# Output projection in four passes of four weight units, and the softmax exponential taken head by head from the score banks

## What is computed

```
h = rms_norm(x); proj = h @ w_in
A  y_conv = gb * conv3(gc * a)                       256 wide
B  y_attn = sliding-window attention, 8 heads of 64  512 wide
     m = max(max(scores), sink); e = exp(scores - m)
     p = e / (sum(e) + exp(sink - m))
C  y_gmlp = gelu(u) * (W_s @ layer_norm(gelu(v)) + b)  256 wide
x = x + concat(rms_norm(A), rms_norm(B), rms_norm(C)) @ w_out
x = x + square(relu(rms_norm(x) @ w_ff1)) @ w_ff2
```

## Time and profile before

| | us |
|---|---|
| median of 3 runs | 2534.04 |
| lowest and highest run | 2528.53, 2535.17 |
| the profiled execution | 2527.28 |
| its span, first to last instruction | 2525.3 |
| PE busy in the span | 2421.5 |
| DVE busy | 1244.2 |
| ACT busy | 609.3 |
| POOL busy | 115.0 |

### The profile page before, as it was taken

One profiled execution on the slowest core, in us unless ns is written; L12 is line 12 of the kernel. 1 busy time (PEld: TensorE's weight loads), 2 busy tenths in 40 slices (PEclk: granted clock), 3 DMA queues, 4 the chain that ended last, 5 costly groups with the idle time before them and its releaser, 6 DMA issues.

```text
span 2525.3 us, 35462 instructions
## 1 busy us (share of the span) xinstructions
PE 2421.5 (96%) x13094; PEld 2138.9 (85%) x13094; DVE 1244.2 (49%) x2221; ACT 609.3 (24%) x1281; POOL 115.0 (5%) x223
## 2 busy tenths in 40 slices
PE   7998998999999999999989998899999999999998
PEld 6987776988998899889888876679899889988996
DVE  5236755444444444444462477464444444444446
ACT  4123412321222122212231234133122212221222
POOL 4010000000000000000020100010000000000001
PEclk9999998999999999999999998999999999999999
DMA  5111001111111111111020011001111111111111
GB/s 159 35 30 42 28 16 34 51 42 43 50 33 38 45 50 33 39 44 58 17 66 26 31 42 35 29 22 59 42 50 33 42 42 50 33 42 42 50 34 75
DMA packets 121189, 109.11 MB, mean 43 GB/s; under 512 B 9724, under 2 KB 93216, under 8 KB 121104
## 3 DMA queue, kind: packets, MB, share of 16 engines
q1 hardware_dynamic: 117248, 100.66, 13.3%
q0 software_dynamic: 2704, 3.10, 0.5%
q10 hardware_dynamic: 1152, 4.19, 0.4%
HBM read 102.18 MB, written 5.54 MB: 43 GB/s over the span
## 4 chain that ended last, share of the span: by engine, by line
PE 89%; DVE 5%; DMA 3%; ACT 2%; issue 1%; SPq 0%; POOL 0%; DVEq 0%; ACTq 0%; POOLq 0%
PE ps L1180 28%; PE ps L1182 28%; PE ps L1181 28%; DMA w_raw<-in_w_out 2%; PE ps L1223 1%; DVE w_lo L830 1%; PE ps L1364 1%; PE ps L1327 1%; PE ps L1347 1%; DVE hT_lo L854 0%; DVE hT_lo L964 0%; SPq L343 0%; PE ps L1308 0%; DVE xn L848 0%; ACT w_hi L552 0%
## 5 line engine op out<-in xcount | busy, mean ns | idle before, releaser
L1180 PE MATMUL ps<-hT_hi,w_hi 128*128 128x384 f32 x1824 | 619.1, 339 | 4.2 <-DVE hT_lo L854 4.2
L1181 PE MATMUL ps<-hT_lo,w_hi 128*128 128x384 f32 x1824 | 616.9, 338 | 0.0
L1182 PE MATMUL ps<-hT_hi,w_lo 128*128 128x384 f32 x1824 | 616.8, 338 | 0.0
L1026 DVE TENSOR_TENSOR x<-ps,x 128x512 f32<-128x512 f32 x576 | 398.1, 691 | 299.5 <-PE ps L1182 290.3
L1180 PE MATMUL ps<-w_hi,ff_hi 128*128 128x512 f32 x1152 | 460.5, 400 | 0.0
L1182 PE MATMUL ps<-w_hi,ff_lo 128*128 128x512 f32 x1152 | 455.7, 396 | 0.0
L1181 PE MATMUL ps<-w_lo,ff_hi 128*128 128x512 f32 x1152 | 452.6, 393 | 0.0
L993 DVE TENSOR_TENSOR r_sb<-r_sb 128x384 f32<-128x384 f32 x192 | 107.0, 558 | 556.1 <-ACT r_sb L611 556.1
L1180 PEld LDWEIGHTS ps<-hT_hi,w_hi 128*128 128x128 f32 x1824 | 345.1, 189 | 6.4 <-DVE hT_lo L854 4.6
L1181 PEld LDWEIGHTS ps<-hT_lo,w_hi 128*128 128x128 f32 x1824 | 345.1, 189 | 1.2
L1182 PEld LDWEIGHTS ps<-hT_hi,w_lo 128*128 128x128 f32 x1824 | 344.8, 189 | 0.0
(11 more groups left out here) (164 smaller groups left out, 1717.3 us busy)
## 6 DMA issues: line engine op xcount, KB each, us to landing
w_raw<-in_w_ff SPq DMA_DIRECT2D x256, 256.0 KB
w_raw<-in_w_in SPq DMA_DIRECT2D x56, 256.0 KB
w_raw<-in_w_out SPq DMA_DIRECT2D x32, 256.0 KB
out<-xn SPq DMA_DIRECT2D x9, 512.0 KB, 2.6
x<-in_x_prompt ACTq DMA_DIRECT2D x7, 512.0 KB, 10.5
w_raw<-in_w_in SPq DMA_DIRECT2D x16, 128.0 KB
gN<-in_w_norm SPq DMA_DIRECT2D x2, 512.0 KB, 6.9
gN<-in_w_norm POOLq DMA_DIRECT2D x2, 512.0 KB, 3.9
```

What stands on the lines that cost most here:

```text
L1026: V.tensor_tensor(xv, ps[:, 6 + n, :], xv, ALU.add).then_inc(x_added.sem, 1)
L1180: pe.matmul(out, sh, mh, start=first, stop=False)
L1181: pe.matmul(out, sh, ml, start=False, stop=False)
L1182: return pe.matmul(out, sl, mh, start=False, stop=last)
```

## The change

The projection is cut by groups and column halves: first the groups A and C ("sides", two units each) of column half 0 for all tiles, then those of half 1, then group B ("attn", four units) of half 0, then of half 1. The units are laid out in this order, so that each part uses four consecutive units. `project_out` is replaced by `side_rows` and `attn_rows` on TensorE and by `add_sides` and `add_attn` on VectorE. The order around the last query tiles is written out anew; the splits of units 44 to 47 come after the adds of side tile 5, the others one by one behind later adds. The last part runs with the second norm. The norm's banks change, and `ff1(0)` takes groups 0 and 1 of its second chunk before it waits for the norm's last tile.

In the softmax VectorE makes `nb = -max/8` instead of subtracting. ScalarE reads the scores from their banks, one call for each head with `nb` as bias, writes `S`, and gives the row sums into `den`. The next scores wait for the exponentials.

```diff
         def norm_banks(w, t):
-            first = (0, 2)[t % 2] if w == 1 else (3, 5)[t % 2]
+            first = (0, 2)[t % 2] if w == 1 else (6, 4)[t % 2]
...
-                        w = HEADS * P if t < TS else DEC_BATCH * KEYS_S
+                        w = P if t < TS else KEYS_S
                         act.wait_ge(*s_sub.at(t))
-                        nc.scalar.activation(S[:, t % 2, 0:w], S[:, t % 2, 0:w], ACT.Exp, scale=SC).then_inc(
-                            *exp_done.tick((t, 0)))
+                        for h in range(HEADS):
+                            nc.scalar.activation(S[:, t % 2, h * w:(h + 1) * w],
+                                                 ps[:, 3 + h // 4, (h % 4) * w:(h % 4 + 1) * w], ACT.Exp,
+                                                 bias=nb[:, h:h + 1], scale=SC,
+                                                 accum_out=den[:, h:h + 1]).then_inc(*exp_done.tick((t, h)))
                         nc.scalar.activation(es[:], sd[:], ACT.Exp, scale=SC).then_inc(*exp_done.tick(t))
                     if i == TS:
 
                         copy_qT(TS)
+                    if i == T + 1:
                         split(range(U_OUT + 4, U_OUT + 8))
...
-                V.tensor_tensor(s_view(t, w), v, by_head(mx[:], w), ALU.subtract)
+                V.tensor_scalar(nb[:], mx[:], -SC, None, ALU.mult)
                 V.tensor_tensor(sd[:], sink[:, kind, :], mx[:], ALU.subtract).then_inc(*s_sub.tick(t))
...
-                link(V.tensor_reduce(den[:].rearrange("p (b h) -> p b h", b=2), s_view(t, w), AX_X, ALU.add))
```

VectorE, after the query tiles:

```diff
+                add_sides(0, 0)
+                softmax_max(TS)
+                add_sides(0, 1)
+                mixed_rows(TS - 2)
+                value_rows(TS - 1)
+                add_sides(0, 2)
+                softmax_norm(TS)
+                add_sides(0, 3)
+                mixed_low(TS - 2)
+                group_scale(TS - 3)
+
+                mixed_rows(TS - 1)
+                add_sides(0, 4)
+                mixed_low(TS - 1)
+                group_scale(TS - 2)
+                add_sides(0, 5)
+                split(range(U_OUT + 4, U_OUT + 8))
+
+                mixed_rows(TS)
+                add_sides(0, 6)
+                mixed_low(TS)
+                group_scale(TS - 1)
+                add_sides(0, 7)
+                group_scale(TS)
+                add_sides(0, TS)
+
+                for t in range(T):
+                    add_sides(1, t)
+                    if 1 <= t <= 4:
+                        split([U_OUT + 8 + t - 1])
+                for t in range(T):
+                    add_attn(0, t)
+                    if 1 <= t <= 4:
+                        split([U_OUT + 12 + t - 1])
                 for t in range(T + 2):
-                    if t == TS:
-                        split(range(U_FF, U_FF + 2))
                     if t < T:
-                        project_out(1, t)
+                        add_attn(1, t)
                     if 1 <= t <= T:
                         normalise(2, t - 1)
                     if t >= 2:
                         norm_low(2, t - 2)
-                    if t == TS:
-                        split(range(U_FF + 2, U_FF + 4))
+                    if 2 <= t <= 5:
+                        split([U_FF + t - 2])
```

TensorE, in `scores`, and the new helpers:

```diff
-                    pe.wait_ge(*s_sub.at(t - 1))
+                    pe.wait_ge(*exp_done.at(t - 1))
...
+            def out_bank(q):
+                if q >= 2:
+                    pe.wait_ge(*out_acc.at(q - 2))
+                else:
+                    pe.wait_ge(*(qn_raw, qT_done)[q].at(TS))
+                return ps[:, (0, 2)[q % 2], :]
+
+            def side_rows(n, t):
+                if n == 0:
+                    pe.wait_ge(*mix_lo.at(t))
+                for grp, ks in enumerate(((0, 1), (6, 7))):
+                    q = side_index(n, t, grp)
+                    ins = rows_by_cols(out_bank(q), t, U_OUT + 4 * n, ks, at=2 * grp)
                     if t < TS:
                         ins.then_inc(*out_full.tick(q))
+
+            def attn_rows(n, t):
+                q = attn_index(n, t)
+                ins = rows_by_cols(out_bank(q), t, U_OUT + 8 + 4 * n, (2, 3, 4, 5), at=0)
```

TensorE, after the query tiles:

```diff
+                q_turn(TS)
+                scores(TS)
+                side_rows(0, 0)
+                values(TS - 2)
+                p_turn(TS - 1)
+                group_sums(TS - 3)
+                for t in (1, 2, 3):
+                    side_rows(0, t)
+
+                values(TS - 1)
+                p_turn(TS)
+                group_sums(TS - 2)
+                side_rows(0, 4)
+                side_rows(0, 5)
+
+                values(TS)
+                group_sums(TS - 1)
+                side_rows(0, 6)
+                group_sums(TS)
+                side_rows(0, 7)
+                side_rows(0, TS)
+
+                for t in range(T):
+                    side_rows(1, t)
+                for t in range(T):
+                    attn_rows(0, t)
                 for t in range(T + 2):
                     if t < T:
-                        project_out(1, t)
+                        attn_rows(1, t)
                     if t >= T:
 
                         g = t - T
-                        pe.wait_ge(*out_acc.at(out_index(1, TS, 2)))
+                        pe.wait_ge(*out_acc.at(attn_index(1, TS)))
                         pe.wait_ge(*norm_lo.at((2, 3 * g + 2, 1)))
                         ff1(0, groups=(g,), chunks=(0,))
                     if t >= 2:
                         norm_turn(2, t - 2)
                 pe.wait_ge(*norm_lo.at((2, TS - 1, 1)))
+                ff1(0, groups=(0, 1), chunks=(1,))
                 pe.wait_ge(*norm_lo.at((2, TS, 1)))
-                ff1(0, groups=(2,), chunks=(0,))
-                ff1(0, chunks=(1,))
+                ff1(0, groups=(2,))
```

More of the change, by code:

```diff
@@ L285, in tile, with side_index, attn_index @@
             return slice(t * P, (t + 1) * P)
-        def out_index(n, t, grp):
-            return (n * T + t) * 3 + grp
+        def side_index(n, t, grp):
+            return (n * T + t) * 2 + grp
+        def attn_index(n, t):
+            return 4 * T + n * T + t
         def y_count(b, t, n):
@@ L415, in _ @@
                     load(vs[64:80, b, :], v_sb[16 * b:16 * b + 16, TS, :], vs_in, "last")
-                for n in range(2):
-                    for k in range(KD):
-                        i = real(U_OUT + n * KD + k)
-                        cols = slice(n * 512, n * 512 + 512)
-                        if 2 <= k < 6:
-                            src = w_out[bass.ds(l, 1), 256:768, cols].rearrange(
-                                "l (g h d) e -> h (l g) d e", g=2, h=G4)[k - 2]
-                        else:
-                            src = out_rows[bass.ds(l * D + k * P, P), cols]
-                        unit(i, 0, raw[:, i % RAW, :], src)
+                for part in range(2):
+                    for n in range(2):
+                        for j in range(4):
+                            i = real(U_OUT + 8 * part + 4 * n + j)
+                            cols = slice(n * 512, n * 512 + 512)
+                            if part == 1:
+                                src = w_out[bass.ds(l, 1), 256:768, cols].rearrange(
+                                    "l (g h d) e -> h (l g) d e", g=2, h=G4)[j]
+                            else:
+                                src = out_rows[bass.ds(l * D + (0, 1, 6, 7)[j] * P, P), cols]
+                            unit(i, 0, raw[:, i % RAW, :], src)
                 w1_units(real(ids_of_w1(0)), 0, 0)
@@ L966, in mixed_low, with add_rows, add_sides, add_attn @@
                 last.then_inc(*mix_lo.tick(t))
-            def project_out(n, t):
-                for grp in range(3):
-                    q = out_index(n, t, grp)
-                    unit = U_OUT + 8 * n + (1, 5, 7)[grp]
-                    if n == 0 and t == TS:
-                        split(range(U_OUT + 8 + (0, 2, 6)[grp], U_OUT + 8 + (2, 6, 8)[grp]))
-                    dve.wait_ge(*(out_full.at(q) if t < TS else released(unit)))
-                    dve.wait_ge(*rg_done.at(t))
-                    if q >= 1:
-                        dve.wait_ge(*out_acc.at(q - 1))
-                    V.scalar_tensor_tensor(x[:, t, n * 512:n * 512 + 512], ps[:, (0, 2)[q % 2], :],
-                                           rG[:, t, grp:grp + 1], x[:, t, n * 512:n * 512 + 512], ALU.mult,
-                                           ALU.add).then_inc(*out_acc.tick(q))
+            def add_rows(n, t, q, grp, unit, ready):
+                dve.wait_ge(*(out_full.at(q) if t < TS else released(unit)))
+                dve.wait_ge(*rg_done.at(t))
+                if ready is not None:
+                    dve.wait_ge(*out_acc.at(ready))
+                xv = x[:, t, n * 512:n * 512 + 512]
+                V.scalar_tensor_tensor(xv, ps[:, (0, 2)[q % 2], :], rG[:, t, grp:grp + 1], xv, ALU.mult,
+                                       ALU.add).then_inc(*out_acc.tick(q))
```

(29 more changed lines are left out.)

87 lines of the change are left out of this document (26 added, 61 removed).

## The result

The changed kernel took 2488.69 us as the median of 4 runs (2485.01 to 2494.01); the kernel before took 2532.84 us in 4 runs beside it. The ratio is 0.983, with a 95% interval of 0.981 to 0.9849: faster by 1.7%. The profiled execution took 2487.94 us, against 2527.28 before: 39.3 us less, where 38.8 was forecast. In a later comparison the changed kernel took 2492.13 us (2490.85 to 2493.58), ratio 0.984 (0.9827 to 0.9852).

A forecast was written before the change was run, and what follows sets the result against it. TensorE, busy 96% of the span, bounds the kernel; only its idle time and half clock can be won. Removing 29.9 us a layer less 10.5 of new losses nets 38.8: 2488.5 profiled, median 2495, range 2479 to 2508.

The forecast's parts named there:

- my bounds of 2.3 and 3.9: ScalarE's eight exponential calls a tile: 2.3 us with overlap, 3.9 without; the middle, 3.1, was taken.
- tightest query copy: Query loop: the exponential ends 1.1 us later, the tightest copy's slack is 0.68, so TensorE waits 0.45 once a layer.
- last query copy, beyond before: Last query tile: TensorE already waited for this copy, and that wait grows by 1.15 us a layer.
- (a): Group sums of tile 8 wait for VectorE's late group scale of tile 7: 2.7 us idle, 1.7 more of clock.
- (b): Last pass with the second norm: VectorE and ScalarE rounds outlast TensorE's tiles; 3.1 us lost, 0.8 more of clock.
- 6.9 + 5.6 - 5.0: Half clock: 6.9 and 5.6 us won in the two layers; new losses a layer 1.7 behind group sums, 0.8 before feed-forward.
- Over 10 us to spare: Projection: whole passes cover both w_out transfers with over 10 us to spare, so the 43.1 us of waits go.
- Rival 2: A weight transfer stays open, for instance units 48 to 51 at the attention pass: 13 us a layer back, 2521; chance 0.05.
- rival 1: The new waits don't form because VectorE runs a little ahead: gain 27 us a layer, 2480; chance 0.10.
- Rival 3: TensorE stays at half clock through the last pass: net -3 us a layer, 2540; chance 0.05 together with Rival 4.
- Rival 4: Eight exponential calls cost far more; gain gone at 6.3 us a tile, 2534 or more; chance 0.05 together with Rival 3.
- Rival 5: TensorE's wait is not for the weights, so the change does not do what it says: about 2534; chance 0.04.

The follow-up runs named there:

- first kernel: Changed kernel with the old softmax put back, so the new projection order alone: 2484.81 us, ratio 0.9814.
- ninth kernel: Changed kernel with the second norm's banks and the order of the first feed-forward products put back as before: 2496.38 us, ratio 0.9864.
- second kernel: Kernel before with only the exponential taken head by head, in the old projection order: 2523.51 us, ratio 0.9966.
- fourth kernel: Changed kernel with the first feed-forward units split in two pairs early in the last pass, not one behind each of tiles 2 to 5: 2488.63 us.
- tenth kernel: New order, old softmax, group scales earlier, feed-forward splits early, first side product and query copy moved before the last scores: 2464.87 us, ratio 0.9735.
- sixth kernel: Changed kernel with each head's exponential cut into two calls of 64 columns, sums joined by VectorE: 2522.78 us, ratio 0.9954.
- seventh: Changed kernel with VectorE's splits of units 44 to 47 after the adds of side tile 8 instead of 5: 2515.32 us, ratio 0.9933.
- third kernel: Changed kernel with VectorE's group scales of tiles 7 and 5 ahead of the low parts of tiles 8 and 6: 2484.75 us, ratio 0.981.
- fifth: Changed kernel with side product 0 before the last scores and the last query copy before the exponential of tile 7: 2482.79 us, ratio 0.9802.
- eleventh: Changed kernel, exponential by heads kept, with group scales earlier, feed-forward splits early, side product and query copy before the last scores: 2468.97 us, ratio 0.9758.

## Why the prediction was right, point by point

**What was removed.** A transfer in the open, twice a layer, each with half clock behind it: the 43.1 and 4.2 us went, 3.1 us of waits for adds are left, and the first kernel shows that the order alone does it. The banks' part is shown by the ninth kernel: 2.1 us a layer, and 4.3 or 7.7 us by the medians, which come from other comparisons.

**The exponential.** Taken 3.1 us a tile, measured 2.76, between my bounds of 2.3 and 3.9. The middle, 0.39 a call, was slightly high: a call is 0.37 us long, its accumulator read starts 0.26 us after it and the next call 0.10 after that, which makes 0.345 from call to call over the eight. The estimate of 0.39 a call by the Trainium skill (ScalarE: Activation LUTs, What ACT_TABLE_LOAD costs) with the row's 0.09 for the read was over by the same 0.05. The wait at the last scores, forecast 1.15 longer, is 1.09 longer (2.46 against 1.37), and the tightest query copy costs 0.29, forecast 0.45. Only the worth of the edit in the old order was wrong: there too the wait at the last scores grew by 1.09 us, but the larger wait behind it fell by 3.8 and 3.4 us, as the second kernel shows. I had looked for VectorE's saving in the query loop only, and not in the chain behind the transfer.

**The new waits.** In idle time a layer:

| place | forecast | measured, first layer |
|---|---|---|
| tightest query copy | 0.45 | 0.29 |
| last query copy, beyond before | 1.15 | 1.09 |
| group sums, tile 8 (a) | 2.7 | 2.42 |
| group sums, tile 6 | 0.6 | 0.38 |
| three shorter ones | 0.45 | 0.22 |
| last pass (b) | 3.1 | 1.93 |
| sum | 8.45 | 6.33 |

The last pass is the one term that is clearly off. I had a round of VectorE and ScalarE at 4.41 us with a split and 3.80 without. ScalarE's sums of squares give the rounds:

```profile
411.54 1.06 ACT L573 ACTIVATE xn<-x 128x1024 f32<-128x1024 f32 x1 [1.61 <-DVE x L993]
...
415.80 1.06 ACT L573 ACTIVATE xn<-x 128x1024 f32<-128x1024 f32 x1 [1.61 <-DVE x L993]
...
424.30 1.06 ACT L573 ACTIVATE xn<-x 128x1024 f32<-128x1024 f32 x1 [1.61 <-DVE x L993]
427.95 1.06 ACT L573 ACTIVATE xn<-x 128x1024 f32<-128x1024 f32 x1 [1.52 <-DVE x L993]
```

That is 4.25 with a split and 3.65 without: 0.15 less a round, over six rounds 0.9 of the 1.2 us. The shape was right, the sum of the steps read from the earlier trace rows slightly long. That the splits make the waits is shown by the fourth kernel.

**The clock.** Forecast 1.7 behind (a) and 0.8 behind the last wait; there was 1.7 and none in the first layer, and in the second 3.4 and none. Behind the last query copy, for which I had set nothing, 1.7 and 3.4 us were lost, where the kernel before lost 3.3 and 1.7. Added up as busy time times one less the granted clock, in windows of 1 us over each layer's middle 320 us, the loss was 13.2 and 10.7 us before and 7.6 and 10.1 after: 6.2 us gained where my terms give 6.9 + 5.6 - 5.0 = 7.5. The missing 1.3 is mostly one loss of 1.7 us behind a wait of 2.26 us at 200.29, ahead of all that was changed; the kernel before has that wait too and lost nothing behind it. Behind like waits the loss came out as 1.7, 3.4 or 4.4 us in different executions of one kernel's layers. This term was a guess that held; what decides between the sizes stays open.

**Cover of the transfers.** "Over 10 us to spare" was wrong, without harm. I took a load of four units from the chain, 13.5 us, as the price of any four. The kernel before had two units of group B and two others in each such four; the four-part order has all four of B together, and these take 4 x 5.34 = 21.4 us. In the changed kernel ScalarE and VectorE reach them so:

```profile
351.41 0.63 ACT L556 ACTIVATE w_hi<-w_raw 128x512 fp32r<-128x512 f32 x1 [4.57 <-DMA w_raw<-in_w_out]
...
357.75 0.63 ACT L556 ACTIVATE w_hi<-w_raw 128x512 fp32r<-128x512 f32 x1 [5.71 <-DMA w_raw<-in_w_out]
```

```profile
362.23 0.68 DVE L836 TENSOR_TENSOR w_lo<-w_raw,w_hi 128x512 fp32r<-128x512 f32 x1
```

Unit 51 is there at 357.7, not 346, and VectorE comes to it at 362.23: its high part is done 3.9 us before that. The deadline is the place of the split in VectorE's program, not TensorE's first use near 372, since all later adds stand behind the split. Rival 2, which I gave 5 in 100, was this close; moving the splits of units 44 to 47 by three tiles brought it about, at 2515 us against the 2521 that I had worked out for it. No kernel here has the old order with loads from rows that lie together, so what these loads alone would give back to the kernel before is not shown.

**The other rivals.** The waits formed at every place that I had walked to, so rival 1 fell; VectorE's saving did not keep any of them away. They go when the places are moved, as the tenth kernel shows. Rival 3 did not come: the last pass ran at clock 1.00 with 1.93 us of pauses. Rival 4's mechanism is the sixth kernel: 4.6 us for the calls cost 31 us. I had put the point at which the whole gain is gone at 6.3 us a tile; with 31 us lost between 2.76 and 4.6 us, and 10.7 left (2533.49 - 2522.78), I estimate it nearer 5.2 by drawing that line on, since I counted idle time and left out the clock behind it. Rival 5 fell with the first kernel and the seventh, in which the waits for the adds come back with the loads.

**The sum.** The profiled pair agrees with it to 0.5 us, which is partly luck. The new waits cost 2.1 us a layer less than forecast, 4.2 in all, and the clock gave 1.3 less: that would make 38.8 + 4.2 - 1.3 = 41.7 us, and 39.3 was measured. What is missing lies in the two long feed-forward stretches, behind all that was changed: by 1 us windows the changed kernel idles and loses less clock there by 2.8 and 3.5 us, and is shorter by only 0.7 and 1.6. What takes the other 4 us there stays open. By layer, the first feed-forward product should not have come 19 us earlier, as I wrote, but some 16.4 (19.4 - 2.1 - 1.7 + 0.8): the wait for the last low part and the half clock behind it lie after this product in the kernel before, as does the 0.8 for the clock behind the last wait here, and I had counted all of them ahead of it. Measured, from the query transposes on, were 20.9 and 16.0 us. That the 21.0 of the first layer looks like my 19 is luck: the waits gave 1.5 us more than forecast, and behind the last query copy 1.7 us of clock were lost instead of the 3.3 before; in the second layer it was 3.4 instead of 1.7. The median came out 6.3 us below the forecast of 2495 for another reason: I added the 6.8 us by which the profiled execution of the kernel before lay under its median, and that of the changed kernel lies only 0.8 under its own.

## What to carry to other kernels

When a reordered stage gathers all units of one kind, price the kind and not the mean: look up each load's own start-to-landing spacing and DMA share before calling a transfer covered, and take as its deadline the place where an in-order engine first touches it, not the place where the product uses it. When an engine is one step late once in a stage, move the instruction that others wait for ahead of those that nobody waits for; a few such lines, moved together, were worth another 20 us here by the medians of the first and tenth kernels, on two chips, where the large reordering won 47 beside the kernel before. A softmax edit that shifts work from VectorE to ScalarE is worth what the later engine of the two costs TensorE at that place, so measure it again after the order around it has changed.

## What the runs showed of the hardware

- A load of 256 KB whose source is two pieces of 64 rows went at 49 GB/s on 0.13 of the DMA engines' time, 5.34 us a unit; loads of the same size from 128 rows together let the same four land some 20 us earlier. The kernel before has two such units in each of the two fours of the earlier trace rows, by that spacing an estimated 10.7 of their 13 us.
- An exponential with a bias from a column, read from a score bank, and with its accumulator read, starts every 0.345 us at 128 columns and every 0.29 us at 64. From the two, an estimate is some 0.235 us for the call and 0.055 for each 64 columns.
- How long TensorE waits does not alone say whether half clock follows, nor for how long. Between the last query tile and the feed-forward, waits of 2.2 to 2.5 us were followed by 4 to 11 us near half clock (one of 2.22 us in the sixth kernel's query loop by 14), but one of 2.41 us (fourth kernel, second layer) by none, and two of 2.10 us by none in the ninth kernel, where the kernel before lost 1.7 and 1.6 us behind the same wait. Waits of 1.33 us before the feed-forward were followed by none in any run that has them, and those of 1.53 and 1.57 us behind the late split by none; but waits of 1.13 us before the group sums cost 1.7 us in each layer of the third kernel, and those of 1.37 us before the last scores 3.2 us in the first kernel. Those of 0.8 us in the fifth and eleventh kernels were followed by none.
